# Moving the search for selected tokens between attention jobs in a two-layer hybrid encoder

## The reference

```python
score = jnp.einsum('bqh,bqhs->bqs', wblk, jax.nn.relu(dots)).astype(jnp.float32)
score = jnp.where(causal[None], score, -jnp.inf)
_, sel = lax.top_k(score, topk)
ks = gather(k, sel)
vs = gather(v, sel)
s = jnp.einsum('bqhd,bqkd->bhqk', qblk, ks) * (d ** -0.5)
```

## Time and profile before

| | us |
|---|---|
| median of 3 runs | 2682.22 (2681.3 to 2686.01) |
| the profiled execution | 2681.9 |
| its span, first to last instruction | 2680.1 |
| TensorE matmuls busy | 2606.7 (97%) |
| VectorE busy | 1816.1 (68%) |
| ScalarE busy | 1226.3 (46%) |
| GpSimd busy | 1245.4 (46%) |

### The profile page before, as it was taken

The page is one execution under the profiler, slowest core; times in us unless marked ns, Lnnn a source line. Parts: engine busy times, 40 slices in busy tenths (PEclk is TensorE's granted clock), DMA queues, the critical chain, the costliest instruction groups (busy, mean ns, idle before and its releaser), DMA issues.

```text
span 2680.1 us, 36990 instructions
## 1 busy us (share of the span) xinstructions
PE 2606.7 (97%) x12480; PEld 2043.2 (76%) x12480; DVE 1816.1 (68%) x3426; ACT 1226.3 (46%) x2463; POOL 1245.4 (46%) x1010
## 2 busy tenths in 40 slices
PE   8999999999999999999999999999999999999997
PEld 7788567768887878787787885676787788787876
DVE  3788786735968283754958887776359673838458
ACT  2566544442343534535435665444423435345453
POOL 5533700014575675756364346001155757657551
PEclk9999999999999999999999999999999999999999
DMA  5312334623442405142142123355325233241512
GB/s 160 88 48 51 86 83 94 134 102 102 155 148 110 142 24 203 57 147 86 64 133 67 48 58 80 83 111 123 112 89 187 104 124 128 80 157 47 175 58 83
DMA packets 117011, 276.68 MB, mean 103 GB/s; under 512 B 16186, under 2 KB 25338, under 8 KB 110394
## 3 DMA queue, kind: packets, MB, share of 16 engines
q1 hardware_dynamic: 107384, 248.99, 31.4%
q10 hardware_dynamic: 9440, 25.33, 2.6%
HBM read 194.67 MB, written 25.39 MB: 82 GB/s over the span
## 4 chain that ended last, share of the span: by engine, by line
PE 39%; DVE 5%; POOL 3%; issue 1%; ACT 1%; DMA 1%; SPq 1%; ACTq 0%; DVEq 0%; POOLq 0%
PE ps L1466 3%; PE ps L1626 3%; PE ps L1625 3%; PE ps L1624 3%; PE ps L1245 2%; PE ps L1247 2%; PE ps L1246 2%; PE ps L1655 2%; PE ps L1657 2%; PE ps L1656 2%; POOL wlo L1206 2%; PE ps L1519 1%; PE ps L1517 1%; PE ps L1518 1%; PE ps L1585 1%
## 5 line engine op out<-in xcount | busy, mean ns | idle before, releaser
L1206 POOL TENSOR_TENSOR wlo<-block,whi 128x512 fp32r<-128x512 f32 x252 | 348.2, 1383 | 259.8 <-ACT whi L1721 255.7
L1206 POOL TENSOR_TENSOR wlo<-wraw,whi 128x512 fp32r<-128x512 f32 (+2 forms) x240 | 317.6, 1324 | 232.5 <-ACT whi L1721 219.8
L1204 POOL CAST whi<-wraw 128x512 fp32r<-128x512 f32 (+2 forms) x152 | 106.3, 700 | 597.9 <-DMA wraw<-in_w_out 284.0
L1721 ACT ACTIVATE whi<-block 128x512 fp32r<-128x512 f32 x252 | 158.4, 631 | 373.0 <-PE ps L1626 169.9
L1655 PE MATMUL ps<-whi,x_place 128*128 128x512 f32 x784 | 311.1, 397 | 11.6 <-POOL wlo L1206 7.7
L2473 DVE TENSOR_TENSOR x_place<-hidden,x_place 128x512 fp32r<-128x512 f32 x196 | 234.9, 1240 | 125.6 <-ACT x_place L1946 123.6
L1657 PE MATMUL ps<-whi,x_place 128*128 128x512 f32 x784 | 310.7, 396 | 0.0
L1656 PE MATMUL ps<-wlo,x_place 128*128 128x512 f32 x784 | 308.1, 393 | 0.0
L1863 ACT ACTIVATE probT<-ps 128x512 f32<-128x512 f32 (+2 forms) x456 | 203.4, 456 | 215.9 <-PE ps L1450 66.1
L1466 PE MATMUL ps<-probT,raw 128*65 128x512 f32 (+2 forms) x720 | 259.7, 443 | 0.0
L1245 PE MATMUL ps<-whi,xhi 128*128 128x512 f32 (+1 forms) x640 | 244.6, 382 | 1.8 <-POOL wlo L1206 1.7
(11 more groups left out here) (279 smaller groups left out, 6593.4 us busy)
## 6 DMA issues: line engine op xcount, KB each, us to landing
x_place<-x_sums SPq DMA_DIRECT2D x48, 1024.0 KB, 5.4
block<-in_w_up SPq DMA_DIRECT2D x120, 256.0 KB, 3.8
wraw<-in_w_in SPq DMA_DIRECT2D x80, 256.0 KB, 2.7
slot<-q_part SPq DMA_DIRECT2D x72, 256.0 KB
slot<-k_part SPq DMA_DIRECT2D x72, 256.0 KB
wraw<-in_w_out SPq DMA_DIRECT2D x64, 256.0 KB, 2.7
down_raw<-in_w_down SPq DMA_DIRECT2D x64, 256.0 KB, 7.7
wraw<-in_w_up SPq DMA_DIRECT2D x48, 256.0 KB, 2.8
```

The source lines that it names most:

```text
L1206: nc.gpsimd.tensor_tensor(lo, loaded, hi.bitcast(F32), ALU.subtract).then_inc(S["w_lo"], 1)
```

## The change

Searches and selections of tiles 2, 3 and 4 take place in other jobs. The code of `find`, `select` and `between` is as before.

```diff
-FIND_AT = {4: [0], 5: [1], 6: [2], 7: [3], 9: [4], 13: [5]}
-SELECT_AT = {4: [0], 5: [1], 6: [2], 9: [3], 12: [4], 14: [5]}
+FIND_AT = {4: [0], 5: [1], 7: [2], 9: [3], 11: [4], 13: [5]}
+SELECT_AT = {4: [0], 5: [1], 8: [2], 10: [3], 12: [4], 14: [5]}
```

## The result

The changed kernel took 2705.61 us (median of 4 runs, 2702.92 to 2706.54), the kernel before 2682.2 beside it (4 runs). The ratio is 1.0082, with a 95% interval of 1.007 to 1.0094: slower by 0.8%, +23.4 us. The forecast was slower, 2697.0, within 2692 to 2704, so the direction was right and the size too small by 8.6 us. The profiled execution is the shortest of the four, 2702.9 us with a span of 2701.1: +21.0 us over before's.

A forecast was written before the change was run, and what follows sets the result against it. TensorE, busy 97% of the span, was taken to bound the kernel; per layer 2.36 + 2.70 + 2.78 − 0.33 = 7.51 us, over two layers +15.0, giving 2697.0 us, range 2692 to 2704.

The forecast's parts named there:

- Which waits grow, and by how much: Turns ending jobs 8, 10, 11 wait for line 2337: +2.36, +2.70, +2.78 us, making gaps of 2.70, 3.04, 3.15.
- Job 7's gain of 0.33: Job 7 gets find 2 for find 3, so its 0.68 us gap shrinks by 0.33, to 0.35.
- job 9's of 0: Job 9's VectorE work falls 3.04 us, but no TensorE gap stood there, so gain 0.
- Job 6's gain of 0: Job 6 loses 4.47 us of VectorE work; the 0.41 us saved is waited at the next gap, for a DMA.
- Nothing won back after a gap: TensorE recovers 0 after each new gap; at most 0.6 us a gap, 3.5 us in six.
- The clock: Rival: TensorE's clock falls in each of six new gaps, 1.2 us each, +7 us to 2704; chance 0.07.
- The price of the rival: Slow matmuls at the kernel's start, 16 to 19 us: a slow spell costs about 1.2 us.
- Rival C: Turns in jobs 8, 10, 11 reached later, so blocks hide and gains stay: −3.7 us, 2678.3; chance 0.05.
- Rival B: Part recovered, after gaps or by job 6's earlier stack DMA: 11.5 to 12 us, 2693.5; chance 0.08.
- Forecast: The whole kernel slower by 15.0 us, 2697.0 (2694 to 2700 for itself); chance 0.80.
- A: Rival: clock falls in each new gap in attention, six of 1.2 us, +7 us to 2704; chance 0.07.

The follow-up runs named there:

- filled: Changed kernel with eight more 128x512 matmuls, read by nobody, on TensorE ahead of the turns ending jobs 8, 10 and 11: 2695.38 us, ratio 1.0041.
- find4_late: Kernel before with find 4 alone moved, from job 9 to job 11: 2691.51 us, ratio 1.0027.
- dose1: Kernel before with one more 1.25 us VectorE multiply ahead of the output in jobs 8, 10 and 11: +6.8 us, ratio 1.0023.
- step11_after: Changed kernel with step 10 of jobs 4 to 11 barred to Q/K turns, which slip by one step: 2690.99 us, ratio 1.0034.
- dose3: Kernel before with three more 1.25 us VectorE multiplies ahead of the output in jobs 8, 10 and 11: +35.7 us, ratio 1.0132.
- turns_moved: Changed kernel with pairs 4, 5 and 6 of the Q/K turns begun later (9/0, 11/0, 12/0): 2691.7 us, ratio 1.0028.
- order_before: Kernel before with VectorE's `between` block two steps later in every job, behind output and turn: 2700.25 us, ratio 1.0069.
- dose2: Kernel before with two more 1.25 us VectorE multiplies ahead of the output in jobs 8, 10 and 11: +22.4 us, ratio 1.0082.
- spread_after: Changed kernel with the Q/K turns reordered, steps 10 and 11 of jobs 4 to 11 barred to them: 2691.54 us, ratio 1.0028.

## Why the prediction was right in its waits and wrong in its time

- **Which waits grow, and by how much: right.** Each gap came within 0.01 us (2.71, 3.04, 3.14 for 2.70, 3.04, 3.15), the blocks that were moved kept their durations, and filled shows that this part alone is 7.84 us a layer.
- **Job 7's gain of 0.33, job 9's of 0: right.** The gap is 0.34 for 0.35, and find4_late, which relieves job 9 alone, gained nothing there.
- **Job 6's gain of 0: right in layer 0, 0.9 us short in layer 1.** In layer 0 the gap behind it took over the 0.41 us and ended, as before, with ScalarE's copy behind the stack's DMA (0.63 us longer). In layer 1 it grew by 1.34 us, 2.33 for 0.99, since that DMA came later there: 0.9 us more than the 0.41 us saved at the gap before it, so 0.9 us that the sum did not have.
- **Nothing won back after a gap: right.** dose1 and filled give the stretch to within 0.04 us of the sum.
- **The clock: this is the step that failed.** The sum put it at nothing; it was a rival with a chance of 0.07 and 1.2 us a gap, and it was the case. The runs put in its place 1.6 us a spell, with four spells in the six gaps of the profiled execution: 15.0 + 4 × 1.6 = 21.4, and the profiled execution is at +21.0. That it comes so close is in part luck, since the stretches alone are +22.15 and the rest of the kernel gave back 1.1, with two spells fewer than before's execution has between the layers. All six would make +24.6; the median of +23.4 lies between. Whether the other three executions had more spells is not known: only one is profiled, and their mean clocks (0.993, 0.994 and 0.994 beside its 0.994) are too coarse to tell.
- **The same in executions without a trace.** The kernel before was timed 55 times beside the experiments, and its time goes with its mean clock: a median of 2682.5 us at 0.997 (30 executions), 2683.9 at 0.996 (16), 2686.7 at 0.995 (5), 2689.0 at 0.994 (2) and 2681.5 at 0.998 (2). So the low time differs from one execution of a kernel to the next and moves its time, and no single profile gives a kernel's price exactly.
- **Why I undervalued it.** I wrote that no gap in the trace of before shows the fall, as all are shorter than the new ones. That was a reading of attention alone. Between the layers the same trace has three spells (from 1339.6, 1360.1 and 1407.9 us), and a window of 1050 us hides them: 545 to 1595 reads 1.00. Kernel before, TensorE and the window around it:

```profile
1407.95 0.69 PE L1348 MATMUL ps<-ik,iq 96*128 96x384 f32 x1 [2.30 <-DMA iq<-iq_part]
1408.44 0.63 PE L1245 MATMUL ps<-whi,xhi 128*128 128x512 f32 x1
```

```profile
1406.00:1412.00 6.00, 4.04 (x11) 3.35 (x12) 1.44 (x3) 1.24 (x3) 0.96 (x1) 0.72 0.83 212
```

  A gap of 2.30 us, shorter than all three of the new ones, with the clock low behind it: 0.72 over 6 us, 3.4 us at the low level. That row makes a spell behind each new gap a case to count with, and the sum 2682 + 15 with up to 6 × 1.6 on top, 2697 to 2707.
- **The price of the rival.** It was taken from the start of the kernel, 1.2 us for 3 us of slow matmuls. The spells in attention are 3.4 us long and cost 0.47 of that.
- **Rival C (not slower)** did not come: TensorE was free for job 8's turn at 406.59 us, in before at 408.00, so it was earlier there and waited, as argued. Rival B did not come either, as nothing was won back.
- **A slip in the chances.** Forecast, A and B add up to 0.95, not to the 0.94 given; it changes no conclusion.

## What to carry to other kernels

Ask of a block of work on a helper engine not how long it is but what stands right behind it in that engine's order, and who waits for that: 5.5 us in job 9 cost nothing, 2.4 us in job 8 cost 2.4. When a change lengthens TensorE's gaps, and here spells stood behind single gaps from 1.87 us up, add the clock to the sum as a range, and look for its price in the trace of before wherever the granted clock is below 1 in narrow windows, not in the stage of the change alone. A gap that can't be closed can be filled: eight matmuls that nobody reads, into a free bank, cost no time of their own here (stretches +7.83 and +7.86 for 7.84) and kept the clock up.

## What the runs showed of the hardware

- Behind TensorE's gaps of 0.83 to 1.28 us (filled, six) and 1.60 to 1.62 us (dose1, six), and of 1.67, 2.01 and 2.10 us (step11_after, six) no spell. Elsewhere in the traces single gaps of 1.87 us (step11_after), 1.91 (dose3, at 290.56), 2.02 and 2.22 (turns_moved) and 2.30 us (before) had one, and single gaps of 2.33 us (after, at 1716.69), 2.37 (dose1, at 1622.79) and 2.56 us (order_before, at 1416.13) had none. Behind 2.71 to 3.16 us it was 12 of 16 (after, dose2, find4_late, turns_moved), behind 4.11 to 4.17 us 6 of 6 (dose3). So between 1.9 and 3.2 us the length alone does not decide: in after the job 8 gap of 2.71 us had a spell in layer 1 and none in layer 0. What else does is not shown.
- A spell can stand behind shorter gaps that lie close together: before, at the start of layer 1, TensorE ran only transposes around and between gaps of 0.98 and 0.90 us, and the clock was 0.72 over the 6 us from 1338, again 3.4 us low. No run separates the part of the transposes from that of the gaps.
- At half the clock each us would lose 0.5 us if TensorE alone set the pace. In these jobs it lost 0.46 to 0.49 us.
- A DMA of 4 KB, issued from ScalarE's queue while SP's copies of stacks were in flight, held TensorE for up to 2.69 us (spread_after, layer 1, at 1705.57, 5.21 us after its issue). TensorE's longest wait for such a write in before is 0.6 us. The copies as the cause are not shown, as said above.
